# A three-buffer conditioning pipeline with interleaved context-projection blocks in the first stage

## The chip, the cores and the metric

The kernel runs on one core of a Trainium2 chip. The metric is the device time of one execution in microseconds (us): for the kernel before, the median of 3 runs is 3599.07 us (3596.9 to 3612.06). About 0.5% of that, 18 us, is what a comparison of this kernel can tell from no change.

## The reference, cut to what matters

The program computes two blocks of a network, one behind the other, in float32. Only the very beginning of the first block is touched by the change:

```python
def ada_params(cond, w, b):
    mod = jax.nn.silu(cond) @ w + b
    return jnp.split(mod, 3, axis=-1)
...
sh_l, sc_l, g_l = ada_params(c, ada_w[layer], ada_b[layer])
sh_c, sc_c, g_c = ada_params(c_ctx, ada_w[layer], ada_b[layer])
xm_l = x_lat * (1.0 + sc_l) + sh_l
xm_c = x_ctx * (1.0 + sc_c) + sh_c
...
proj = xm @ w_in        # of it, the first 512 columns of v belong to the first stage
```

Shift and scale (2048 each, for two conditioning vectors) come from a product with `ada_w` and are applied to the 256 tokens of `x` and the 256 of the context; then the modulated tokens are multiplied by `w_in`.

## The kernel before

**Precision and units.** All weights come from HBM in units of 1 MB (128 partitions x 2048 float32) through a ring of four slots, loaded by SyncE in a fixed order. A unit is used as two halves of 1024 columns. Each half is split into two parts that TensorE multiplies: ScalarE copies it, rounded, into `unit_hi` (`hb[b]`), VectorE writes what is left, ring minus `unit_hi`, into `unit_lo` (`lb[b]`). There are NBUF = 4 pairs of such buffers.

**The first stage.** It has 72 halves, listed in FIRST; x is a half's place in that list. 64 of them are conditioning halves ("A", called A0, A1, ... by their place x): two row blocks of `ada_w`, for which TensorE does four matmuls of 512 columns with the conditioning vectors as the stationary operand (`ada_half`, L799 and L801), into bank 4 or 5. The other eight are context halves ("L", called C30, C38, ... by their place): two row blocks of `w_in`'s v columns, 8 blocks of 128 x 128 each. For every block TensorE does six matmuls of 256 columns (`both_sets`, L824): tokens and context, and high and low parts, into banks 0 to 3. Before, the context halves stand at x = 30, 38, 47, 55 and 68 to 71.

**The chain of a group.** The conditioning comes in four groups of 4 x 128 features, 16 halves each. When a row of a group is complete, ScalarE copies it out of its bank (`ada_row`, L1393); with both there, TensorE turns the rows to columns (`ada_turn`, 16 weight loads and matmuls at L815, ahead of place ENDS[g] + 3, for the last group within a context half), VectorE adds the bias (`modulated`, L2045 and L2046), ScalarE applies scale and shift to four chunks of tokens and four of context (`x_scaled`, L1403), writes their high parts (`x_hi`, L1411), and VectorE their rests (`x_lo`, L1929). Only then may TensorE take the context halves of that group (semaphore `xm_lead`).

**What sets the order.** Every engine's program is written out by hand and runs in its own order; the engines meet in semaphores. ScalarE walks over x: for each half it waits for the ring's slot and for TensorE to be done with the buffer (`half_done`), then writes `unit_hi`. At fixed places the row copies, `x_scaled` and `x_hi` stand between. VectorE walks over x too: it waits for `hi_done` >= x + 1 and writes `unit_lo`, with `modulated` and `x_lo` at fixed places between. TensorE waits for `lo_done` >= x + 1 for the half x. Since these are counters, a half is ready only when all ahead of it in the list are split as well. In before, half x uses buffer x % 4, and `half_done` is raised by TensorE at the end of each half in the same order. SyncE loads a ring slot again when VectorE has written both rests of its unit. After the stage come the gates (two halves, 16 blocks in bank 7) and the rest of v, whose low parts GpSimd makes.

The line in ScalarE's helper that binds a half to the buffer's last user:

```python
for f in halves:
    b = (2 * n_static + f) % NBUF
    act.wait_ge(half_done, 2 * n + f + 1)
    act.activation(hb[b][:], ring[slot][:, f * HALF:(f + 1) * HALF], ACT.Copy).then_inc(hi_done, 1)
```

`half_done` starts at NBUF, so that half x waits for x - 4 to be done.

## Time and profile before

| | |
|---|---|
| median of 3 runs | 3599.07 us |
| lowest, highest | 3596.9, 3612.06 us |
| the profiled execution | 3602.43 us, of it the span 3600.6 us |
| TensorE (PE) busy | 3487.5 us, 97% |
| VectorE (DVE) busy | 2387.4 us, 66% |
| ScalarE (ACT) busy | 1619.1 us, 45% |
| GpSimd (POOL) busy | 1587.1 us, 44% |
| the first stage | from the start to 152 us |

Times in the views are microseconds from the start of the span. PE is TensorE's matmuls and PEld its weight loads; in the timeline an entry gives start, duration, engine, line of the source, output <- inputs, count, and in brackets how long the engine had been idle and what released it. A matmul's duration in these views is longer than the distance to the next one, since matmuls overlap; the distance of the starts is what a matmul costs. The granted clock (PEclk) is the share of TensorE's full 2.4 GHz.

### The profile page before, as it was taken

How to read it: one execution, taken by the hardware profiler on the slowest of the kernel's cores; microseconds unless marked ns; L12 is line 12 of the kernel's file. 1: busy time of each engine (PE TensorE's matmuls, PEld its weight loads, DVE VectorE, ACT ScalarE, POOL GpSimd, SP SyncE). 2: the span in 40 equal slices, each digit the busy share in tenths (PEclk: the TensorE clock that was granted, in tenths of full speed). 3: DMA queues.
4: the chain of work that ended last, by engine and by line, in shares of the span. 5: the costliest groups of instructions: out<-in, count | busy, mean ns of one | idle time of the engine just before them, and what ended most of it. 6: DMA issues, size and time to landing. Idle time of an engine off the chain costs nothing.

```text
span 3600.6 us, 65963 instructions
## 1 busy us (share of the span) xinstructions
PE 3487.5 (97%) x27080; PEld 3316.3 (92%) x27080; DVE 2387.4 (66%) x3663; ACT 1619.1 (45%) x2143; POOL 1587.1 (44%) x671
## 2 busy tenths in 40 slices
PE   7999998999999999999999999999999999999998
PEld 3799897979998989999999999999999899999998
DVE  7587466884545558364213779778888878788865
ACT  7513433333344444464444434444555444455553
POOL 0247592007264867826889980002333200133336
PEclk9999999999999999999999999999999999999999
DMA  9457661855564444545555555557888555688843
GB/s 354 191 225 265 268 238 59 327 208 213 223 223 147 164 153 148 204 164 188 185 190 196 190 180 195 188 184 256 318 304 313 183 196 197 239 323 302 314 175 129
DMA packets 118129, 784.66 MB, mean 218 GB/s; under 512 B 13488, under 2 KB 13616, under 8 KB 31920
## 3 DMA queue, kind: packets, MB, share of 16 engines
q1 hardware_dynamic: 97056, 703.65, 53.4%
q0 software_dynamic: 18832, 67.94, 4.8%
q10 hardware_dynamic: 2016, 9.87, 0.7%
q8 instruction: 165, 2.70, 0.3%
q14 instruction: 60, 0.49, 0.0%
HBM read 778.49 MB, written 2.10 MB: 217 GB/s over the span
## 4 chain that ended last, share of the span: by engine, by line
PE 83%; DVE 9%; POOL 2%; DMA 2%; ACT 2%; issue 2%; SPq 0%; DVEq 0%; ACTq 0%; POOLq 0%
PE bank L634 45%; PE bank L1236 12%; PE bank L652 6%; PE bank L1238 6%; PE bank L654 3%; DMA ring<-in_w 2%; POOL unit_lo L568 2%; PE bank L706 2%; PE bank L824 1%; PE bank L683 1%; ACT unit_hi L1328 1%; DVE ada_acc L1869 1%; PE bank L1184 1%; DVE unit_lo L1952 1%; PE bank L603 1%
## 5 line engine op out<-in xcount | busy, mean ns | idle before, releaser
L1328 ACT ACTIVATE unit_hi<-ring 128x1024 fp32r<-128x1024 f32 x1204 | 1248.2, 1057 | 1245.6 <-PE bank L634 429.0
L568 POOL TENSOR_TENSOR unit_lo<-ring,unit_hi 128x1024 fp32r<-128x1024 f32 x522 | 1337.8, 2584 | 962.0 <-ACT unit_hi L1328 961.0
L634 PE MATMUL bank<-x_parts,unit_hi 128*128 128x256 f32 (+1 forms) x7328 | 1306.8, 279 | 20.5 <-DVE unit_lo L1952 6.4
L634 PEld LDWEIGHTS bank<-x_parts,unit_hi 128*128 128x128 f32 x7328 | 1132.7, 190 | 27.9 <-issue 11.1
L634 PE MATMUL bank<-x_parts,unit_lo 128*128 128x256 f32 (+1 forms) x3664 | 1017.3, 278 | 0.0
L634 PEld LDWEIGHTS bank<-x_parts,unit_lo 128*128 128x128 f32 x3664 | 696.2, 190 | 0.0
L1236 PE MATMUL bank<-w_r,unit_hi 128*128 128x448 f32 x2048 | 647.4, 374 | 6.0 <-DVE w_r L2933 6.0
L1238 PE MATMUL bank<-w_r,unit_lo 128*128 128x224 f32 x2048 | 544.7, 266 | 0.0
L1236 PEld LDWEIGHTS bank<-w_r,unit_hi 128*128 128x128 f32 x2048 | 385.6, 188 | 38.0 <-DVE w_r L2933 3.8
L1238 PEld LDWEIGHTS bank<-w_r,unit_lo 128*128 128x128 f32 x2048 | 392.2, 192 | 0.0
L2848 DVE TENSOR_TENSOR unit_lo<-ring,unit_hi 128x1024 fp32r<-128x1024 f32 x256 | 313.4, 1225 | 99.9 <-ACT unit_hi L1328 90.9
L525 POOL DMA_INDIRECT pick<-in_ev,expert_idx x64 | 111.9, 1749 | 495.6 <-PE bank L1184 280.5
L652 PE MATMUL bank<-x_parts,unit_hi 128*128 128x448 f32 x1024 | 329.9, 380 | 0.0
L2741 DVE TENSOR_TENSOR unit_lo<-ring,unit_hi 128x1024 fp32r<-128x1024 f32 x224 | 270.6, 1221 | 86.4 <-ACT unit_hi L1328 86.0
L654 PE MATMUL bank<-x_parts,unit_lo 128*128 128x224 f32 x1024 | 271.2, 265 | 0.0
L525 POOL DMA_INDIRECT pick<-in_eu,expert_idx x64 | 116.0, 1812 | 238.9 <-DVE expert_dot L2860 203.2
L652 PEld LDWEIGHTS bank<-x_parts,unit_hi 128*128 128x128 f32 x1024 | 193.2, 189 | 17.1
L1869 DVE SCALAR_TENSOR_TENSOR ada_acc<-ring,cond,ada_acc 128x2048 f32<-128x2048 f32 x64 | 186.5, 2914 | 29.1 <-DMA ring<-in_w 27.8
L1952 DVE TENSOR_TENSOR unit_lo<-ring,unit_hi 128x1024 fp32r<-128x1024 f32 x130 | 153.4, 1221 | 76.0 <-ACT unit_hi L1328 75.6
L654 PEld LDWEIGHTS bank<-x_parts,unit_lo 128*128 128x128 f32 x1024 | 196.9, 192 | 0.0
L634 PE MATMUL bank<-ry_hi,unit_hi 128*128 128x256 f32 x480 | 133.0, 277 | 0.6 <-issue 0.6
L634 PE MATMUL bank<-ry_lo,unit_hi 128*128 128x256 f32 x480 | 132.6, 276 | 0.0
(484 smaller groups left out, 5782.1 us busy)
## 6 DMA issues: line engine op xcount, KB each, us to landing
ring<-in_w SPq DMA_DIRECT2D x669, 1024.0 KB, 4.9
resid<-in_xT ACTq DMA_DIRECT2D x4, 512.0 KB, 6.5
tmp_ctx<-in_ctxT ACTq DMA_DIRECT2D x4, 512.0 KB, 10.9
sgu_rows<-in_sgr ACTq DMA_DIRECT2D x1, 2048.0 KB, 10.3
rnn_gates<-in_rgw ACTq DMA_DIRECT2D x1, 2048.0 KB, 10.5
out<-resid SPq DMA_DIRECT2D x4, 512.0 KB, 2.6
pick<-in_eu,expert_idx POOLq DMA_INDIRECT x64, 8.0
pick<-in_ev,expert_idx POOLq DMA_INDIRECT x64, 8.1
```

The source lines that it names most:

```text
L525: pool.indirect_dma_start(slots[PICK_SLOT[k]][:], None, A[table][:, :], bass.IndirectOffsetOnAxis(ap=eidx[:, j:j + 1], axis=0), element_of ...
L568: pool.tensor_tensor(lb[b][:], ring[slot][:, f * HALF:(f + 1) * HALF], hb[b][:].bitcast(F32), ALU.subtract).then_inc(lo_done, 1)
L634: mm = pe.matmul(bank[(s.t0 + tile[m]) % TILES][:, 0:cols], w[b][:, (i % 8) * P:(i % 8 + 1) * P], mv[x][:, k, 0:cols], start=(k == 0 and w ...
L652: pe.matmul(two_parts(ps), hb[b][:, (k % 8) * P:(k % 8 + 1) * P], xb[:, :, k, 0:TM], start=(k == 0), stop=(k == KC - 1), skip_group_check= ...
L654: mm = pe.matmul(ps[:, 0:TM], lb[b][:, (k % 8) * P:(k % 8 + 1) * P], xb[:, 0, k, 0:TM], start=False, stop=(k == KC - 1), skip_group_check= ...
L1236: pe.matmul(two_parts(bank[c]), hb[b][:, c * P:(c + 1) * P], x[:], start=first, stop=False, skip_group_check=True)
L1238: return pe.matmul(bank[c][:, 0:TM], lb[b][:, c * P:(c + 1) * P], x[:, 0, :], start=False, stop=False, skip_group_check=True)
L1328: act.activation(hb[b][:], ring[slot][:, f * HALF:(f + 1) * HALF], ACT.Copy).then_inc(hi_done, 1)
L1869: dve.scalar_tensor_tensor(a[:], ring[u % RING][:], col, a[:], ALU.mult, ALU.add).then_inc(plain_done, 1)
L1952: dve.tensor_tensor(lb[b][:], ring[(s.u0 + s.npos[j]) % RING][:, f * HALF:(f + 1) * HALF], hb[b][:].bitcast(F32), ALU.subtract).then_inc(l ...
L2741: dve.tensor_tensor(lb[b][:], ring[(s.u0 + u) % RING][:, f * HALF:(f + 1) * HALF], hb[b][:].bitcast(F32), ALU.subtract).then_inc(lo_done, 1)
L2848: dve.tensor_tensor(lb[b][:], ring[(s.u0 + u) % RING][:, f * HALF:(f + 1) * HALF], hb[b][:].bitcast(F32), ALU.subtract).then_inc(lo_done, 1)
```

## The change

Four things are changed together, all within the first stage.

- The list FIRST: the context halves now stand at x = 28, 37, 46, 55, 64 and 69 to 71. The conditioning halves keep their order.
- The buffers: conditioning halves take turns in buffers 0, 1 and 2; the context halves at 28, 37, 46, 55, 64 and 71 all take buffer 3 (those at 69 and 70 take 1 and 2).
- TensorE's order: FIRST_PE lists its steps. When a context half is met, its eight blocks are put on a list, and behind each following conditioning half TensorE takes one block from it; what is left is done at the end. The eight halves of `[C28]` so lie behind A29 to A36, those of C37 behind A38 to A45, and so on; C64 has four blocks behind A65 to A68 and four after them. The last turn stands ahead of C69's first block.
- The waits on `half_done` follow: FIRST_DONE says as which TensorE completes a half, and `first_buffer_free(x)` which count the buffer's last user gives. ScalarE waits for that count.

The diff, cut to its core:

```diff
-FIRST = (ADA[:30] + [("L", 0, 0, 0)] + ADA[30:37] + [("L", 0, 0, 1)] + ADA[37:45] + [("L", 1, 0, 0)]
-         + ADA[45:52] + [("L", 1, 0, 1)] + ADA[52:] + [("L", g, 0, f) for g in (2, 3) for f in range(2)])
+LEADS = {28: (0, 0), 36: (0, 1), 44: (1, 0), 52: (1, 1), 60: (2, 0)}
+FIRST = []
+for _i, _a in enumerate(ADA):
+    if _i in LEADS:
+        FIRST.append(("L",) + (LEADS[_i][0], 0, LEADS[_i][1]))
+    FIRST.append(_a)
+FIRST += [("L", 2, 0, 1), ("L", 3, 0, 0), ("L", 3, 0, 1)]
+FIRST_BUF, _n = [], 0
+for _kind, _g, _i, _f in FIRST:
+    FIRST_BUF.append(_n % 3 if _kind == "A" else {(2, 1): 1, (3, 0): 2}.get((_g, _f), 3))
+    _n += _kind == "A"
+FIRST_PE, _open = [], []
+for _x, _h in enumerate(FIRST):
+    if _h[0] == "L":
+        _open += [(_x, _i) for _i in range(8 * _h[3], 8 * _h[3] + 8)]
+        continue
+    FIRST_PE.append((_x, None))
+    if _open:
+        FIRST_PE.append(_open.pop(0))
+FIRST_PE += _open
+_last = {_x: _k for _k, (_x, _) in enumerate(FIRST_PE)}
+FIRST_DONE = {_x: _n + 1 for _n, _x in enumerate(sorted(_last, key=_last.get))}
+def first_buffer_free(x):
+    before = [y for y in range(x) if FIRST_BUF[y] == FIRST_BUF[x]]
+    return FIRST_DONE[before[-1]] if before else 0
+TURN_LAST = (2, 8)
...
-            for x, (kind, g, i, f) in enumerate(FIRST):
-                u = x % NBUF
+            for x, part in FIRST_PE:
+                kind, g, i, f = FIRST[x]
+                u = FIRST_BUF[x]
...
-                for i in range(8 * f, 8 * f + 8):
-                    if g == 2 and i == 2:
-                        ada_turn(3)
...
+                if (g, part) == TURN_LAST:
+                    ada_turn(3)
+                mm = both_sets(bank[part % 4], (hb, lb), u, part, (xl, xc), GR * g + part // 4,
+                               g == 0 and part < 4, g == 3 and part >= 12)
+                if part % 8 == 7:
+                    mm.then_inc(half_done, 1)
...
-                            act.wait_ge(half_done, NBUF + ROW_END[g][b] + 1)
+                            act.wait_ge(half_done, NBUF + FIRST_DONE[ROW_END[g][b]])
...
+                    act.wait_ge(half_done, NBUF + first_buffer_free(x))
```

**TensorE, where a context half's blocks end.** Before, TensorE's row at the last matmuls of C30 (buffer 2), the conditioning half A31 (buffer 3) and the start of A32 (buffer 0):

```order
L824 MATMUL bank3<-x_parts_72,unit_hi2_55 128x256
L824 MATMUL bank3<-xc_lo_74,unit_hi2_55 128x256
L824 MATMUL bank3<-x_parts_72,unit_lo2_59 128x256
L824 MATMUL bank3<-xc_hi_73,unit_lo2_59 128x256
L799 MATMUL bank4<-unit_hi3_56,cond_parts_104 4x512 [waits lo_done]
L801 MATMUL bank4<-unit_lo3_60,cond_parts_104 2x512
L799 MATMUL bank4<-unit_hi3_56,cond_parts_104 4x512
L801 MATMUL bank4<-unit_lo3_60,cond_parts_104 2x512
L799 MATMUL bank4<-unit_hi0_53,cond_parts_104 4x512 [waits lo_done]
```

After, TensorE's row at the last block of C28 (buffer 3), A38 (buffer 0) and the first block of C37 (buffer 3 again):

```order
L861 MATMUL bank3<-x_parts_72,unit_hi3_56 128x256
L861 MATMUL bank3<-xc_lo_74,unit_hi3_56 128x256
L861 MATMUL bank3<-x_parts_72,unit_lo3_60 128x256
L861 MATMUL bank3<-xc_hi_73,unit_lo3_60 128x256
L836 MATMUL bank4<-unit_hi0_53,cond_parts_104 4x512 [waits lo_done]
L838 MATMUL bank4<-unit_lo0_57,cond_parts_104 2x512
L836 MATMUL bank4<-unit_hi0_53,cond_parts_104 4x512
L838 MATMUL bank4<-unit_lo0_57,cond_parts_104 2x512
L861 MATMUL bank0<-x_parts_72,unit_hi3_56 128x256 [waits lo_done]
L861 MATMUL bank0<-xc_hi_73,unit_hi3_56 128x256
```

Before, the context half's end is followed by halves whose buffers were free all along; now it is followed by A38, which stands behind C37 in the list of halves, and C37 goes into the buffer that has just been read.

**ScalarE, at the same place.** Before, ScalarE's row at x = 36 to 39 (C38 is the one in buffer 2), with the loads of tokens and the first scaling of group 1:

```order
L1328 ACTIVATE unit_hi0_53<-ring2_51 128x1024 [waits half_done,slot_loaded2]
L1433 DMA resid_61<-in_xT 128x1024
L1434 DMA tmp_ctx_75<-in_ctxT 128x1024
L1328 ACTIVATE unit_hi1_54<-ring2_51 128x1024 [waits half_done,slot_loaded2]
L1328 ACTIVATE unit_hi2_55<-ring3_52 128x1024 [waits half_done,slot_loaded3]
L1328 ACTIVATE unit_hi3_56<-ring3_52 128x1024 [waits half_done,slot_loaded3]
L1403 ACTIVATE tmp_lat_76<-resid_61,mod_64 128x256 [waits x_in1,mod_ready]
```

After, the same stretch of ScalarE (C37 is the one in buffer 3):

```order
L1469 ACTIVATE unit_hi2_55<-ring2_51 128x1024 [waits half_done,slot_loaded2]
L1479 DMA resid_61<-in_xT 128x1024
L1480 DMA tmp_ctx_75<-in_ctxT 128x1024
L1469 ACTIVATE unit_hi3_56<-ring2_51 128x1024 [waits half_done,slot_loaded2]
L1469 ACTIVATE unit_hi0_53<-ring3_52 128x1024 [waits half_done,slot_loaded3]
L1469 ACTIVATE unit_hi1_54<-ring3_52 128x1024 [waits half_done,slot_loaded3]
L1443 ACTIVATE tmp_lat_76<-resid_61,mod_64 128x256 [waits x_in1,mod_ready]
```

The length and kind of the row are the same; the context half has moved ahead by one place and waits for `half_done` of C28 where C38 waited for that of A34.

**ScalarE, at the end of the stage.** Before, ScalarE's row at x = 69 to 71, with the copy of the last conditioning row:

```order
L1328 ACTIVATE unit_hi1_54<-ring2_51 128x1024 [waits half_done,slot_loaded2]
L1328 ACTIVATE unit_hi2_55<-ring3_52 128x1024 [waits half_done,slot_loaded3]
L1393 ACTIVATE ada_rows_103<-bank5 4x512 [waits half_done]
L1328 ACTIVATE unit_hi3_56<-ring3_52 128x1024 [waits half_done,slot_loaded3]
L1403 ACTIVATE tmp_lat_76<-resid_61,mod_64 128x256 [waits x_in3,mod_ready]
```

After:

```order
L1469 ACTIVATE unit_hi1_54<-ring2_51 128x1024 [waits half_done,slot_loaded2]
L1469 ACTIVATE unit_hi2_55<-ring3_52 128x1024 [waits half_done,slot_loaded3]
L1469 ACTIVATE unit_hi3_56<-ring3_52 128x1024 [waits half_done,slot_loaded3]
L1433 ACTIVATE ada_rows_103<-bank5 4x512 [waits half_done]
L1443 ACTIVATE tmp_lat_76<-resid_61,mod_64 128x256 [waits x_in3,mod_ready]
```

The row copy (`ada_rows`), which stood ahead of the high part of x = 71, now stands behind it, and that half now takes buffer 3, which C64 holds.

## Rows read from the trace of the kernel before

**Rows 1.** The page: the span; busy time, share of the span, instructions of TensorE.

```profile
span 3600.6 us, 65963 instructions
...
PE 3487.5 (97%) x27080; PEld 3316.3 (92%) x27080; DVE 2387.4 (66%) x3663; ACT 1619.1 (45%) x2143; POOL 1587.1 (44%) x671
```

**Rows 2.** Timeline of the last turn and the end of the stage, engine by engine.

```profile
128.04 0.49 PE L815 MATMUL bank<-con,ada_rows 4*128 4x4 f32 x3
...
130.03 0.17 DVE L2045 SCALAR_TENSOR_TENSOR mod<-bank,vec 128x8 f32<-128x8 f32 x1 [0.34 <-PE bank L815]
...
130.82 2.07 ACT L1403 ACTIVATE tmp_lat<-resid,mod 128x256 f32<-128x256 f32 x4 [2.39 <-DVE tick L2020]
...
137.05 1.22 DVE L1929 TENSOR_TENSOR xc_lo<-tmp_ctx,xc_hi 128x1024 fp32r<-128x1024 f32 x1
...
152.26 1.06 ACT L1328 ACTIVATE unit_hi<-ring 128x1024 fp32r<-128x1024 f32 x1 [4.32 <-PE bank L824]
```

**Rows 3.** Windows: us, busy us per engine, granted clock, DMA share, GB/s.

```profile
20.00:40.00 20.00, 14.21 (x64) 5.09 (x64) 14.59 (x18) 14.20 (x16) 0.00 (x0) 1.00 1.01 415
...
80.00:100.00 20.00, 16.88 (x90) 8.80 (x88) 15.01 (x14) 12.64 (x14) 0.00 (x0) 0.91 0.77 289
```

**Rows 4.** Waits, 0 to 150 us (SyncE's own last): total us, times, longest.

```profile
DVE unit_lo L2062 <- ACT unit_hi L1328: 31.9, 22, 4.3
...
ACT unit_hi L1328 <- PE bank L824: 17.9, 5, 5.0
...
ACT unit_hi L1328 <- PE bank L801: 10.6, 10, 1.9
...
SPq L463 <- DVE unit_lo L2062: 114.3, 36, 6.4
```

**Rows 5.** Chain that ended last: start us, us, engine, line, count.

```profile
67.28 1.87 PE bank L815 x16
...
104.15 5.46 PE bank L824 x48
```

**Rows 6.** Timeline of TensorE from C30's last matmul into A31.

```profile
63.29 0.28 PE L824 MATMUL bank<-xc_hi,unit_lo 128*128 128x256 f32 x1
63.41 0.40 PE L799 MATMUL bank<-unit_hi,cond_parts 128*4 128x512 f32 x1
...
64.33 0.40 PE L799 MATMUL bank<-unit_hi,cond_parts 128*4 128x512 f32 x1
```

**Rows 7.** Timeline of ScalarE and VectorE after C47 ended at 95.65.

```profile
95.75 1.06 ACT L1328 ACTIVATE unit_hi<-ring 128x1024 fp32r<-128x1024 f32 x1 [4.38 <-PE bank L824]
...
96.71 1.04 ACT L1328 ACTIVATE unit_hi<-ring 128x1024 fp32r<-128x1024 f32 x1
...
96.84 5.78 DVE L2062 TENSOR_TENSOR unit_lo<-ring,unit_hi 128x1024 fp32r<-128x1024 f32 x5 [4.21 <-ACT unit_hi L1328]
```

**Rows 8.** Timeline of group 1's scaling (ScalarE) and rests (VectorE).

```profile
71.22 2.06 ACT L1403 ACTIVATE tmp_lat<-resid,mod 128x256 f32<-128x256 f32 x4
...
79.90 1.99 ACT L1328 ACTIVATE unit_hi<-ring 128x1024 fp32r<-128x1024 f32 x2
...
80.97 1.23 DVE L2062 TENSOR_TENSOR unit_lo<-ring,unit_hi 128x1024 fp32r<-128x1024 f32 x1 [0.67 <-ACT unit_hi L1328]
...
84.39 8.24 DVE L2062 TENSOR_TENSOR unit_lo<-ring,unit_hi 128x1024 fp32r<-128x1024 f32 x7
```

**Rows 9.** Timeline around the first turn: ScalarE, and TensorE's A18.

```profile
37.14 1.04 ACT L1328 ACTIVATE unit_hi<-ring 128x1024 fp32r<-128x1024 f32 x1
38.79 1.06 ACT L1328 ACTIVATE unit_hi<-ring 128x1024 fp32r<-128x1024 f32 x1 [0.60 <-PE bank L801]
...
37.61 0.40 PE L799 MATMUL bank<-unit_hi,cond_parts 128*4 128x512 f32 x1
```

**Rows 10.** Windows of 3.4 us, columns as in Rows 3.

```profile
83.20:86.60 3.40, 1.09 (x5) 0.25 (x4) 3.40 (x4) 2.01 (x3) 0.00 (x0) 0.98 0.84 308
86.60:90.00 3.40, 3.40 (x9) 1.11 (x9) 3.40 (x4) 2.12 (x2) 0.00 (x0) 0.52 0.61 200
```

More of the change, by code:

```diff
@@ L136 @@
 NFIRST = len(FIRST) // 2
+for _b in range(4):
+    assert max(FIRST_DONE[_x] for _x in range(2 * NFIRST) if FIRST_BUF[_x] == _b) <= 2 * NFIRST - 3 + _b
+TURN_LAST = (2, 8)
 class Stage:
@@ L829, in _ @@
             pe.wait_ge(S("cond_lo"), 1)
-            for x, (kind, g, i, f) in enumerate(FIRST):
-                u = x % NBUF
-                for turned in range(NG - 1):
-                    if x == ENDS[turned] + 3:
-                        ada_turn(turned)
-                if kind == "L" and f == 0:
-                    pe.wait_ge(S("xm_lead"), 2 * g + 2)
-                pe.wait_ge(lo_done, x + 1)
+            for x, part in FIRST_PE:
+                kind, g, i, f = FIRST[x]
+                u = FIRST_BUF[x]
                 if kind == "A":
+                    for turned in range(NG - 1):
+                        if x == ENDS[turned] + 3:
+                            ada_turn(turned)
+                    pe.wait_ge(lo_done, x + 1)
                     ada_half(u, g, i, f)
                     continue
-                for i in range(8 * f, 8 * f + 8):
-                    if g == 2 and i == 2:
-                        ada_turn(3)
-                    mm = both_sets(bank[i % 4], (hb, lb), u, i, (xl, xc), GR * g + i // 4,
-                                   g == 0 and i < 4, g == 3 and i >= 12)
-                mm.then_inc(half_done, 1)
+                if part % 8 == 0:
+                    if f == 0:
+                        pe.wait_ge(S("xm_lead"), 2 * g + 2)
+                    pe.wait_ge(lo_done, x + 1)
+                if (g, part) == TURN_LAST:
[4 more added lines that the diff above has]
+                    mm.then_inc(half_done, 1)
             n = PLAN["gates"].n0
@@ L1425, in _ @@
                 u = s0.u0 + x // 2
-                hi(x // 2, (u % RING, u // RING + 1, x // 2), (x % 2,))
+                if x < 2 * NFIRST:
+                    act.wait_ge(slot_loaded[u % RING], 16 * (u // RING + 1))
+                    act.wait_ge(half_done, NBUF + first_buffer_free(x))
+                    act.activation(hb[FIRST_BUF[x]][:], ring[u % RING][:, x % 2 * HALF:(x % 2 + 1) * HALF], ACT.Copy
+                                   ).then_inc(hi_done, 1)
+                else:
+                    hi(x // 2, (u % RING, u // RING + 1, x // 2), (x % 2,))
                 if x == 4:
@@ L2059, in _ @@
                 if x < 2 * NFIRST:
-                    b = x % NBUF
+                    b = FIRST_BUF[x]
                     dve.wait_ge(hi_done, x + 1)
```

## Prediction

> **What bounds the kernel now.** Halves are named by their place x in FIRST: A27 is a conditioning half, C30 a context half of eight blocks. TensorE is busy 97% of the span [rows 1], but the edit touches only the first stage, which ends when the last context half is done: the instruction of ScalarE that waits for it starts at 152.26 [rows 2]. So I read the first 152 us and ask who ends each wait there. In the window from 80 to 100 us TensorE is busy 16.88 of 20 us, DMA at 0.77 [rows 3]: neither is full. In the waits, ScalarE waits 17.9 us for TensorE's context blocks, 10.6 us for its conditioning matmuls, and VectorE 31.9 us for ScalarE [rows 4]. SyncE waits 114.3 us for VectorE to free a slot of the ring: the loads are ahead. The three engines' waits are one loop: TensorE frees a buffer, ScalarE writes its high part, VectorE the rest, TensorE uses it. While TensorE is in a context half the loop stands still for four buffers.
>
> The prices. A context half is 48 matmuls in 5.46 us, so 0.68 us for a block of six, and a turn of rows to columns 1.87 us [rows 5]. A conditioning half is four matmuls 0.23 us apart, 0.92 us, and passing from a block to it costs nothing: 63.29 to 63.41 is a block matmul's own spacing [rows 6]. After a context half ends, the high part starts 0.1 us later and the next 0.96 us after it; VectorE starts 1.1 us after the first and goes on every 1.15 us [rows 7].
>
> Check of these prices on before. From C30 at 57.68 TensorE has 34 conditioning halves (31.3 us), 64 blocks (43.5) and 3 turns (5.6) left: 80.4 us, so 138.1 without any wait. It is done at 152.2. The 14.1 us between are all that a perfect interleave could give back, half-rate clock included.
>
> **The change part by part.** *Interleaving.* TensorE's work is the same; per pair it has 0.92 + 0.68 = 1.60 us, above VectorE's 1.15 and ScalarE's 0.95 for a half. With three buffers for conditioning, a freed one is wanted again 2 x 0.92 + 3 x 0.68 = 3.9 us later, and needs 0.1 + 1.06 + 1.2 = 2.4 us. So inside a run of pairs there is no wait, and the 5 us standstill goes.
>
> *The one buffer for context halves.* This is what I think decides. C37 may be written only when C28's last block is done, and TensorE's order puts that block directly ahead of A38 (the order fence of TensorE). ScalarE takes its instructions in order, so C37's high part and everything behind it (A38, A39, the scalings of group 1) stand still until then; VectorE then splits C37 first, and only then A38. TensorE has nothing else queued but A38. Its hole, by [rows 7]: 0.1 to the high part, 1.1 to the first rest, 2 x 1.15 for both rests: 3.5 us. It occurs at x = 37, 46, 55 and 64, since each context half stands directly behind the end of the one before. At 37 and 55 the sums of `modulated` stand between the two rests, 0.8 us from the first of them to ScalarE's next [rows 2]: 4.3 us there. Sum of holes: 2 x 3.5 + 2 x 4.3 = 15.6 us. In before the same waits were covered by three conditioning halves that were ready.
>
> *ScalarE's scalings, behind the holes at 37 and 55.* They cannot begin before `modulated`, 3.2 us after TensorE's last block. ScalarE's row shows 71.22 for the first scaling and 79.90 for the high part of the half ahead of which the last scaled parts went: 8.7 us [rows 8]. VectorE starts that half's rest at 80.97, then two rests of x, and the next half's rest at 84.39, done at 85.6 [rows 8]; so that is 14.4 us after the first scaling, 17.6 after the last block. Here that is the rest of A44. TensorE, from 4.3 on, has A38 to A43 with six blocks, 9.6 us, to 13.9; so it waits 3.6 us in all on A41 to A44. Before had this too (its loss is in the 14.1), hidden in part by C38. Twice: 7.2 us. Each piece of nine halves from 37 thus takes 17.6 + 2 x 1.6 = 20.8 us, that from 46 (no scaling) 3.5 + 8 x 1.6 + 1.9 = 18.2.
>
> *The tail.* The last conditioning half, A68, now has 5 blocks of C64 behind it. C71 goes into the context buffer too, so its high part waits for C64's end, and on ScalarE the row copy that the last turn needs stands behind C71 (the order fence of ScalarE): 0.1 + 0.95 + 0.6 = 1.7 us of waiting TensorE before the turn. From the turn's start x's rests are ready at 137.05 + 1.22 - 128.04 = 10.2 us [rows 2]; TensorE covers 1.9 + 8 x 0.68 = 7.3 of them with the turn and C69, and waits 2.9 us before C70. Before it had two whole context halves there and no wait. Tail: 4.6 us.
>
> *Three buffers instead of four ahead of x = 28.* There ScalarE waits mostly for DMA, and a cycle of three buffers (1.06 + 1.2 + 0.92 + 0.1 = 3.3 us, 1.1 a half) is still under the 1.26 us in which a half of 0.52 MB arrives at 415 GB/s [rows 3]. The exception is the first turn: A18 comes behind it at 37.61 and ends 0.92 later, at 38.5; with four buffers only A22's high part waited for it, 0.60 us, with three it is A21's, which began at 37.14 [rows 9] and now does at 38.6. The scaling chain behind starts 0.8 us later. Bounds: 0, if VectorE's own queue is what ends last, and 1.5, the whole shift of A21; I take 0.8.
>
> *The start.* A29 is split one cadence (1.15 us) ahead of what was C30: 56.5, with the 0.8 57.3.
>
> Sum for the stage: 57.3 + 36 x 0.92 (33.1) + 64 x 0.68 (43.5) + 3 x 1.87 (5.6) = 139.5, plus waits 15.6 + 7.2 + 4.6 = 27.4: 166.9. Against 152.2: **+14.7 us**, at full clock.
>
> *The clock.* From 83.2 to 86.6 TensorE was busy 1.09 of 3.40 us at a granted 0.98; from 86.6 to 90 it got 0.52, half of 2.4 GHz [rows 10]. At half rate 3.4 us of work lose 1.7. Such costs of before are in its 14.1. After, there are four holes of 3.5 to 4.3 us. Behind those at 37 and 55 the later waits (3.6) take up the loss; behind those at 46 and 64 TensorE is the bound and 1.7 us is lost each; behind the tail's hole I count half of one, 0.8. That is 4.2 us; bounds 0 (none falls on paced work) and 8.5 (five of them).
> The Trainium skill ("TensorE: Matmul & The Clock Gate", "Why this matters for your kernels") says that a longer idle gap between bursts of matmuls sends the clock back to half rate. By that rule, this change, which keeps TensorE fed in small bites but opens four gaps, pays it every time. The row at 83.2 to 90 agrees with it; that every gap of this size does it, no run here shows yet.
>
> After the stage all is released from TensorE's last block, as in before, where VectorE's and ScalarE's next steps stand at 152.26 [rows 2], and the weight ring is full in before [rows 4] and, drained more slowly, in the changed kernel too. So I carry the delay on in full. Forecast: 14.7 + 4.2 = **+18.9 us**. The profiled execution was 3602.43 us (span 3600.6), the median 3599.07; from the median this gives **3618**.
>
> **The rivals.**
> 1. *Holes, but no cost of the clock:* 14.7 us, 3614. For it: from 80 to 100 us, with gaps of several us on TensorE, the clock was still 0.91 in the mean [rows 3], so only some gaps cost anything. Against: [rows 10], where one did.
> 2. *Half rate after every gap, on work that paces:* five stretches of 1.7, 14.7 + 8.5 = 23.2, 3622. For it: the gaps here, with what is light around them, are as bare as the stretch of [rows 10]. Against: the holes at 37 and 55 have slack behind them. The rule of the Trainium skill above would lead here.
> 3. *Not slower: the holes are covered.* If the new context half's high part did not keep ScalarE from running ahead (its buffer free before A38 is wanted), the 15.6 us and some of the scaling waits go. The stage is then 139.5 + 4.6 to 139.5 + 11.8: 144 to 151, that is 1 to 8 us faster, 3591 to 3598. It decides where the last block of a context half stands: one half earlier than the next context half would do. In before the loop's standstill (17.9 us) is real, which speaks for a gain; the order, with no half between, speaks against.
> 4. *Absorbed later:* part of the delay is taken up behind the stage. GpSimd has its first splits earlier than needed there. But they were ready in time before too, so a delay of the whole can't be hidden; if half of it were, 3608.
> 5. *The buffers of x < 28 matter more than I think:* the ring is starved once or twice for want of a freed slot and every later load is late by a half's 1.26 us or two each time, +3 to +5 on top: 3622.
>
> **How the numbers follow.** Forecast (3616 to 3620) 0.45; rival 1 0.25; rivals 2 and 5 0.17; rival 4 0.07; rival 3 0.06. A measurement here can tell about 0.5% (18 us: below 3581 or above 3617) from no change, and my forecast lies just at that bound. Slower by over 0.5%: 0.7 of the forecast (0.31) and rivals 2 and 5 (0.17), 0.48. Within: 0.50. Faster by over 0.5%: even without any wait the stage gives 14 us, so 0.02. The range must hold rival 1 and reach into 2 and 4: 3608 to 3627.
>
> **What would show it.** Four gaps of 3.5 to 4.4 us before a conditioning half on TensorE, each with ScalarE waiting for a block of TensorE just ahead of a high part in the context buffer; the waits of ScalarE for context blocks fewer and shorter than 17.9 us; stage end at 165 to 172 instead of 152.3; a wait of about 3 us before C70; a granted clock near 0.5 in stretches behind the gaps. It is wrong if conditioning halves follow at those four places without a gap (rival 3), if the stage ends at 167 with a clock of 1.0 (rival 1), or if the stage's delay is not found in the total (rival 4).

## The result and the profile after

The changed kernel took **3622.56 us** (median of 6 runs, 3618.64 to 3630.69), the kernel before 3600.81 us in 6 runs beside it: 21.8 us slower, ratio 1.0061 with a 95% interval of 1.0048 to 1.0075. The profiled execution of the changed kernel, 3630.69 us with a span of 3628.8, is the slowest of its six; before's was 3602.43. Places in a trace are those of one execution.

In the section on the change, "the eight halves of C28" behind A29 to A36 are its eight blocks; C28 is one half.

The instructions that answer to the end of the stage: VectorE's copy out of the banks, behind TensorE's last block. Timeline of VectorE, first kernel before, then after; columns as in the timelines above:

```profile
152.26 2.74 DVE L2068 COPY vstage<-bank 128x256 f32<-128x256 f32 x8 [13.99 <-PE bank L824]
```

```profile
175.55 2.74 DVE L2114 COPY vstage<-bank 128x256 f32<-128x256 f32 x8 [11.67 <-PE bank L861]
```

The stage ends 23.3 us later; in before it is the same moment as the instruction of ScalarE at 152.26 in [rows 2]. Then the delay goes through the kernel. One later place, of before and of after, from the views of one source line (instruction and count, duration least/median/most in ns, first and last start):

```profile
L706 PE MATMUL bank<-unit_hi,x_parts x256: 388/392/581, 737.2 to 827.9; 128*128 128x512 f32 x128
```

```profile
L743 PE MATMUL bank<-unit_hi,x_parts x256: 387/392/586, 769.4 to 860.2; 128*128 128x512 f32 x128
```

It is 32.2 us later there, and 28.2 at the end of the span. Nothing is taken up; the few microseconds between these figures are within what single executions of one kernel differ by.

TensorE in the stage, after: every wait of 1 us or more in the 36 pairs, the last turn, and the wait before C70. In brackets how long TensorE stood idle before it and for whom.

```profile
57.32 0.59 PE L836 MATMUL bank<-unit_hi,cond_parts 128*4 128x512 f32 x1 [1.19 <-DVE unit_lo L2108]
...
79.93 0.40 PE L836 MATMUL bank<-unit_hi,cond_parts 128*4 128x512 f32 x1 [4.78 <-DVE unit_lo L2108]
...
92.72 0.39 PE L836 MATMUL bank<-unit_hi,cond_parts 128*4 128x512 f32 x1 [1.32 <-DVE unit_lo L2108]
...
99.70 0.39 PE L836 MATMUL bank<-unit_hi,cond_parts 128*4 128x512 f32 x1 [3.60 <-DVE unit_lo L2108]
...
120.75 0.40 PE L836 MATMUL bank<-unit_hi,cond_parts 128*4 128x512 f32 x1 [4.39 <-DVE unit_lo L2108]
...
133.93 0.39 PE L836 MATMUL bank<-unit_hi,cond_parts 128*4 128x512 f32 x1 [1.63 <-DVE unit_lo L2108]
...
140.91 0.39 PE L836 MATMUL bank<-unit_hi,cond_parts 128*4 128x512 f32 x1 [3.60 <-DVE unit_lo L2108]
...
153.68 1.92 PE L852 MATMUL bank<-con,ada_rows 4*128 4x4 f32 x16 [1.73 <-issue]
...
163.94 0.38 PE L861 MATMUL bank<-x_parts,unit_hi 128*128 128x256 f32 x1 [0.98 <-DVE xc_lo L1975]
```

The four holes stand before A38, A47, A56 and A65. What makes the first of them is read on the two other engines; timeline of ScalarE and VectorE, after (C28's last matmul starts at 74.88):

```profile
75.25 2.95 ACT L1469 ACTIVATE unit_hi<-ring 128x1024 fp32r<-128x1024 f32 x3 [6.45 <-PE bank L861]
76.34 1.23 DVE L2108 TENSOR_TENSOR unit_lo<-ring,unit_hi 128x1024 fp32r<-128x1024 f32 x1 [6.28 <-ACT unit_hi L1469]
...
78.65 2.36 DVE L2108 TENSOR_TENSOR unit_lo<-ring,unit_hi 128x1024 fp32r<-128x1024 f32 x2 [0.42 <-DVE tick L2066]
```

ScalarE stood 6.45 us at C37's high part, for TensorE's block of C28, with A38's behind it. VectorE then splits C37 (76.34), does group 1's `modulated`, and only from 78.65 splits A38, which TensorE takes at 79.93. In [rows 7] the same restart took place with TensorE still fed. The later four of this kind, ScalarE's high parts of C46, C55, C64 and C71, after:

```profile
96.20 3.90 ACT L1469 ACTIVATE unit_hi<-ring 128x1024 fp32r<-128x1024 f32 x4 [5.83 <-PE bank L861]
...
116.46 2.95 ACT L1469 ACTIVATE unit_hi<-ring 128x1024 fp32r<-128x1024 f32 x3 [6.45 <-PE bank L861]
...
137.41 3.90 ACT L1469 ACTIVATE unit_hi<-ring 128x1024 fp32r<-128x1024 f32 x4 [5.83 <-PE bank L861]
...
152.05 1.06 ACT L1469 ACTIVATE unit_hi<-ring 128x1024 fp32r<-128x1024 f32 x1 [4.09 <-PE bank L861]
```

Each follows 0.1 us behind the end of a context half, so they cut the stage into **pieces**: 20.95, 20.26, 20.95 and 14.64 us, and 23.5 from the last to the copy at 175.55. The experiments are read by these pieces.

The waits from 0 to 150 us, after (those of [rows 4]):

```profile
ACT unit_hi L1469 <- PE bank L861: 24.6, 4, 6.5
...
SPq L500 <- DVE unit_lo L2108: 132.4, 35, 8.8
```

And the clock, windows of after, columns as in [rows 3]: the start of the pairs, the hole before A38, what follows it, what follows the holes before A47, A56 and A65, and the last turn with C69.

```profile
57.00:63.40 6.40, 6.08 (x21) 3.87 (x22) 3.80 (x5) 2.40 (x3) 0.00 (x0) 0.50 1.01 407
...
74.50:80.00 5.50, 0.72 (x7) 0.53 (x6) 3.12 (x8) 4.69 (x7) 0.00 (x0) 1.00 0.32 107
80.00:84.00 4.00, 4.00 (x14) 2.30 (x15) 2.23 (x2) 4.00 (x7) 0.00 (x0) 0.57 0.91 320
...
100.90:104.60 3.70, 3.70 (x17) 2.57 (x16) 2.25 (x2) 1.95 (x2) 0.00 (x0) 0.54 0.84 325
...
121.00:124.00 3.00, 3.00 (x12) 1.94 (x11) 2.06 (x2) 3.00 (x7) 0.00 (x0) 0.56 0.93 358
142.00:145.50 3.50, 3.50 (x16) 2.40 (x15) 2.35 (x2) 1.47 (x2) 0.00 (x0) 0.53 0.91 356
154.00:160.00 6.00, 6.00 (x40) 5.98 (x40) 1.00 (x6) 3.58 (x8) 0.00 (x0) 0.72 0.53 178
```

Each of the four holes is followed by a stretch near 1.2 GHz (0.5 of full). A shorter one follows the wait of 1.73 us before the last turn: the 0.72 of the last row is the mean of 6 us, and 3 of these, from 155.7 to 158.7, ran at 0.50. The four holes agree with the rule of the Trainium skill that the prediction weighed ("TensorE: Matmul & The Clock Gate", "Why this matters for your kernels"). The wait of 1.73 us is shorter than the gaps that it speaks of.

### The profile page after: what moved, and what is told of

Read it like the earlier page. It is cut to its first block, busy times and chain, and to the rows that moved or that the text cites. A ratio compares the mean times of both kernels' runs of the same rounds, so it can differ in the third digit from the quotient of the medians.

```text
span 3628.8 us, 65963 instructions
## 1 busy us (share of the span) xinstructions
PE 3499.3 (96%) x27080; PEld 3330.2 (92%) x27080; DVE 2384.0 (66%) x3663; ACT 1619.6 (45%) x2143; POOL 1585.0 (44%) x671
## 4 chain that ended last, share of the span: by engine, by line
PE 83%; DVE 9%; ACT 2%; POOL 2%; issue 2%; DMA 2%; DVEq 0%; SPq 0%; ACTq 0%; POOLq 0%
PE bank L671 46%; PE bank L1276 11%; PE bank L689 6%; PE bank L1278 6%; PE bank L691 3%; POOL unit_lo L605 2%; DMA ring<-in_w 2%; PE bank L743 2%; PE bank L861 1%; PE bank L720 1%; PE bank L1224 1%; DVE ada_acc L1915 1%; DVE unit_lo L2108 1%; PE bank L640 1%; DVE unit_lo L1998 1%
## 5 line engine op out<-in xcount | busy, mean ns | idle before, releaser
L1368 ACT ACTIVATE unit_hi<-ring 128x1024 fp32r<-128x1024 f32 x1132 | 1174.9, 1058 | 1213.3 <-PE bank L671 432.6
L671 PEld LDWEIGHTS bank<-x_parts,unit_hi 128*128 128x128 f32 x7328 | 1135.7, 191 | 27.7 <-issue 10.9
```

The source lines that it names most:

```text
L671: mm = pe.matmul(bank[(s.t0 + tile[m]) % TILES][:, 0:cols], w[b][:, (i % 8) * P:(i % 8 + 1) * P], mv[x][:, k, 0:cols], start=(k == 0 and w ...
```

## The experiments

All are compared with runs of the kernel before on the same chip; these had medians of 3600.81 to 3603.89 us, so it is the ratios that compare. "Stage end" is the start of the copy `vstage`, 152.3 in before and 175.6 in the changed kernel. It is read from one execution of each: the changed kernel and e7, one program up to the last row copy, differ by 2.2 us in one piece of the stage and by 0.9 the other way in another. So 2 or 3 us in this column alone show nothing. A change of order or of buffers is made on the changed kernel.

| kernel | order | buffers for A + for C | stage end, us | median, us | ratio to before, 95% |
|---|---|---|---|---|---|
| before | eight in a row | 4 shared | 152.3 | 3600.81 | 1 |
| changed | one block a half | 3 + 1 | 175.6 | 3622.56 | 1.0061 (1.0048 to 1.0075) |
| e1 | one block | 3 + 2 | 155.5 | 3606.01 | 1.0017 (1.0006 to 1.0028) |
| e2 | two blocks | 3 + 1 | 159.8 | 3609.72 | 1.0023 (1.0011 to 1.0034) |
| e3 | one block, holes filled, 14 fillers | 3 + 1 | 176.6 | 3632.15 | 1.0084 (1.0065 to 1.0102) |
| e5 | one block | 4 + 1 | 171.4 | 3621.16 | 1.0051 (1.0033 to 1.0069) |
| e6 | one block, holes filled, 8 fillers | 3 + 1 | 169.9 | 3624.15 | 1.0065 (1.0046 to 1.0083) |
| e7 | one block, row copy first | 3 + 1 | 173.8 | 3625.23 | 1.0066 (1.0043 to 1.0089) |
| e8 | eight in a row | 3 + 1 | 167.5 | 3619.20 | 1.0043 (1.0026 to 1.0060) |
| e9 | one block, C68 to C71 at the end | 4 + 2 | 149.3 | 3600.52 | 0.9989 (0.9978 to 1.0000) |
| e10 | eight in a row | 4 + 1 | 150.9 | 3605.18 | 1.0001 (0.9992 to 1.0010) |

**A second context buffer (e1).** A fifth pair of buffers lies where nothing else is live in this stage; C37 and C55 use it.

```diff
-    FIRST_BUF.append(_n % 3 if _kind == "A" else {(2, 1): 1, (3, 0): 2}.get((_g, _f), 3))
+    FIRST_BUF.append(_n % 3 if _kind == "A" else {(2, 1): 1, (3, 0): 2, (0, 1): 4, (1, 1): 4}.get((_g, _f), 3))
...
+        hb.append(zone("unit_hi4", 98, [P, HALF], F32R))
+        lb.append(zone("unit_lo4", 102, [P, HALF], F32R))
```

> The changed kernel with a second buffer pair for context halves: C28, C46, C64 in buffer 3, C37 and C55 in a new buffer 4; conditioning halves stay in three, TensorE's order is untouched. Theory (the single buffer makes ScalarE hold up everything behind a context half until the one before is read): no idle stretch of 3.6 to 4.8 us ahead of A38, A47, A56 and A65; the 16.4 us of them go, and with them one or two of the half-rate stretches behind (1.6 us each): the stage ends at 155 to 160 us instead of 175.5, the whole takes 3602 to 3607 us. Rival 1 (three buffers for conditioning halves are too few) and rival 2 (taking blocks one by one is what costs, by its switching or by the clock): the stage still ends at 172 to 176, the whole stays at 3618 to 3625.

The stage ended at 155.5. TensorE of e1; the waits behind the first two context halves; 1.08 and 1.62 stand once more at 111.89 and 119.09, and none else of 1 us or more between 60 and 125:

```profile
80.19 0.39 PE L838 MATMUL bank<-unit_hi,cond_parts 128*4 128x512 f32 x1 [1.08 <-DVE unit_lo L2110]
...
87.39 0.39 PE L838 MATMUL bank<-unit_hi,cond_parts 128*4 128x512 f32 x1 [1.62 <-DVE unit_lo L2110]
```

No hole is left, and the stage ends 20.1 us before that of the changed kernel (about 1 of these is the start: the first turn of the pairs, group 1's, is at 68.92 instead of 69.89). In this order the single context buffer made the holes, not the interleaving as such.

**Two blocks a half (e2).** The blocks of a context half are done after four conditioning halves, so that its buffer is free four halves before the next wants it.

```diff
-    if _open:
-        FIRST_PE.append(_open.pop(0))
+    FIRST_PE += _open[:2]
+    del _open[:2]
```

> The changed kernel with its buffers, but TensorE takes two blocks behind a conditioning half, not one, so that a context half is read through four conditioning halves ahead of the next one. Theory: the buffer is free 3.7 us of work earlier, which is as long as the hole: holes gone, the stage ends at 155 to 161, the whole 3602 to 3608 us. Rival 1 (three conditioning buffers): 3618 to 3625, since nothing of that changes. Rival 2 (small bites): part of it at most, 3612 to 3620.

Stage end 159.8, 15.8 us less than the changed kernel: the holes go with the one buffer kept. That is the second way to the same end, and shows that the hold time of the buffer decides. The total, 3609.7, lies above the 3602 to 3608 expected. The waits that stay between 70 and 130 us are six, of 0.6 to 2.3 us.

**Fillers in the holes (e3, then e6).** Before the wait of A38, A47, A56 and A65 TensorE multiplies constants into a bank that nobody reads: 14 times in e3, 8 times in e6.

```diff
+                    if x in (38, 47, 56, 65):
+                        keep(14, 7)
                     pe.wait_ge(lo_done, x + 1)
```

> The changed kernel with 14 matmuls of no use (256 columns, about 0.22 us each at full clock, 3.1 us) into the unused bank 7 ahead of TensorE's waits for A38, A47, A56 and A65: they fill the holes and change no buffer. Theory, its clock term: the half-rate stretches behind these holes (0.57 at 80 to 84, 0.54 at 100.9 to 104.6, 0.53 at 142 to 145.5) go; behind A47 and A65 they are on the path with 1.6 us each, so the stage ends 3 us earlier, at 172 to 173, and the whole takes 3618 to 3620 us instead of 3622.6. If the clock costs nothing there: no change. If the matmuls last longer than the hole: slower.

The 14 took 5.9 us, 0.42 each, where I had counted on 0.22; the holes are 3.6 to 4.8, so the fillers overran them. TensorE of e3, and two windows behind the fillers (columns as above):

```profile
74.97 6.21 PE L819 MATMUL bank<-con 128*128 128x256 f32 x28
80.82 0.58 PE L836 MATMUL bank<-unit_hi,cond_parts 128*4 128x512 f32 x1
```

```profile
80.00:84.00 4.00, 4.00 (x24) 2.76 (x23) 2.22 (x2) 4.00 (x7) 0.00 (x0) 1.00 0.87 330
...
100.00:105.00 5.00, 5.00 (x29) 3.65 (x28) 2.66 (x3) 1.37 (x3) 0.00 (x0) 1.00 0.86 315
```

The clock stays at 1.00 where the changed kernel had 0.57 and 0.54, with the same work there: the idle time ahead had sent it down. In time e3 settles little, since the overrun ate the gain: its pieces are 20.95, 20.98, 20.97 and 15.36 us. Its median is 31 us above before for a stage that ends 24.3 later; the interval of its ratio begins at 23.4 us, and whether there is more than scatter behind the stage stays open. So the fillers were cut to 8.

> As the run with 14 useless matmuls, but with 8: one measured 0.42 us there, so 14 of them (5.9 us) overran the hole by 1 to 2 us each, while the work behind them ran at a full clock. 8 are 3.4 us, within the holes of 3.6 and 4.4 to 4.8 us. Theory, its clock term: all four stretches behind the holes run at full clock and cost 1.1 to 1.6 us less each, also behind A38 and A56, where the prediction had counted on slack: the stage ends at 169 to 172 us instead of 175.5, the whole takes 3615 to 3619 us. If the clock term is only the 3 us predicted: 172 to 173, 3619. If the clock falls all the same: 175, 3622.

With 8, TensorE waits 1.33 us behind the fillers of A38 and 0.94 behind those of A56, and not at all behind the other two. The clock is 1.00 from 60 to 140 us; one window, and ScalarE's high parts of C37, C46, C55, C64 and C71 in e6:

```profile
120.00:140.00 20.00, 17.06 (x97) 11.49 (x96) 13.41 (x13) 12.82 (x15) 0.00 (x0) 1.00 0.62 229
```

```profile
73.03 2.95 ACT L1471 ACTIVATE unit_hi<-ring 128x1024 fp32r<-128x1024 f32 x3 [6.45 <-PE bank L861]
...
94.02 3.90 ACT L1471 ACTIVATE unit_hi<-ring 128x1024 fp32r<-128x1024 f32 x4 [5.86 <-PE bank L861]
...
112.74 2.95 ACT L1471 ACTIVATE unit_hi<-ring 128x1024 fp32r<-128x1024 f32 x3 [6.45 <-PE bank L861]
...
133.70 3.90 ACT L1471 ACTIVATE unit_hi<-ring 128x1024 fp32r<-128x1024 f32 x4 [5.84 <-PE bank L861]
...
146.78 1.06 ACT L1471 ACTIVATE unit_hi<-ring 128x1024 fp32r<-128x1024 f32 x1 [4.09 <-PE bank L861]
```

The pieces are 20.99, **18.72**, 20.96 and **13.08**. Those with a scaling (from C37 and from C55) are as long as with the half rate, 20.95: there the scalings' chain sets the length and the loss of the clock is hidden. The other two are shorter by 1.54 and 1.56 us: what a drop cost in these executions where nothing hides it (e7, further down, has a dearer one). This is what the prediction had said of each; the expectation above, which hoped for a gain behind A38 and A56 too, was wrong. The stage ends at 169.9, 5.7 us earlier: 3.1 from these two pieces, 0.4 from the last, and 2.2 that are there at 73.03 already, ahead of any filler. So it is by luck that 169.9 falls into the 169 to 172 expected. The total doesn't show it: 3624.15 was measured where 3615 to 3619 was expected, and by the interval (17 to 30 us above before) it is no better than the changed kernel (17 to 27).

**Four conditioning buffers (e5).** Is it the third or the fourth buffer of the conditioning halves that matters?

```diff
-    FIRST_BUF.append(_n % 3 if _kind == "A" else {(2, 1): 1, (3, 0): 2}.get((_g, _f), 3))
+    FIRST_BUF.append(_n % 4 if _kind == "A" else {(2, 1): 1, (3, 0): 2, (3, 1): 3}.get((_g, _f), 4))
```

(and the fifth pair of e1)

> The changed kernel with four buffers (0 to 3) for conditioning halves and a fifth, new one for C28, C37, C46, C55 and C64; the last three context halves take 1, 2 and 3. TensorE's order is untouched. Theory: the holes stay at 3.6 to 4.8 us, since the context halves still share one buffer; what goes is 0.8 us at the first turn and the 1.7 us ahead of the last turn (C71's high part waits for A68, not for C64): the stage ends 2 to 4 us earlier than 175.5, the whole takes 3617 to 3621. Rival 1 (three buffers are too few): most of the loss goes, 3600 to 3608.

TensorE of e5 at the holes:

```profile
76.86 0.59 PE L838 MATMUL bank<-unit_hi,cond_parts 128*4 128x512 f32 x1 [4.78 <-DVE unit_lo L2110]
...
96.66 0.59 PE L838 MATMUL bank<-unit_hi,cond_parts 128*4 128x512 f32 x1 [3.60 <-DVE unit_lo L2110]
```

The four holes are 4.78, 3.60, 4.39 and 3.60 us, the same to the hundredth. They ask only when the context buffer comes free, not how many the others have. The stage ends 4.2 us earlier. Its start gives 3.1 of these (group 1's turn is at 66.77 instead of 69.89), but only about 1 by the buffer: a conditioning half waited for at 55.05 in the changed kernel begins at 54.10. The rest is the clock of the first pairs (0.93 from 57.0 to 60.2, for 0.50), which e7 will show to differ between executions. The wait before the last turn, which e5 doesn't have, gives more, and the piece from C37's end to C46's takes some back (21.15 us for 20.26).

**The row copy ahead of C71 (e7).**

```diff
-                        if x == ROW_END[g][b] + 4:
+                        if x == min(ROW_END[g][b] + 4, 2 * NFIRST - 1):
```

> The changed kernel, but ScalarE's copy of the last conditioning row stands ahead of C71's high part, not behind it, as in the kernel before. Theory: TensorE's idle 1.73 us ahead of the last turn goes, the wait ahead of C70 grows by some tenths since VectorE has C71's rest to write first; the stage ends 1 to 1.7 us earlier, at about 174 us, too little for the total to show (3621). Rival: the copy was not what ended last there, and the 1.73 us stay.

TensorE's wait of 1.73 before the last turn is gone, and that before C70 is 3.09 instead of 0.98. From A65 to the stage's end it takes 34.25 us (139.59 to 173.84) where the changed kernel takes 34.64 (140.91 to 175.55). The row copy did gain something: C70 begins 10.6 us after C64's end (161.15) instead of 12.0 (163.94). But C70 and C71 then take 12.7 us instead of 11.6, for the clock falls behind the longer wait; windows from C70 on, first e7, then the changed kernel:

```profile
161.10:164.60 3.50, 3.45 (x17) 3.46 (x18) 0.00 (x0) 0.37 (x1) 3.50 (x2) 0.54 0.00 0
```

```profile
163.90:167.40 3.50, 3.46 (x29) 3.47 (x30) 0.00 (x0) 0.35 (x1) 3.50 (x2) 1.00 0.00 0
```

So removing the first wait made the second long enough to cost 1.1 of the 1.4 us gained. The stage end is 1.7 us earlier, as expected, but by luck. Only 0.4 of it is the tail; the wait before C70 grew by 2.1 us and not by tenths.

The rest lies ahead, where e7 and the changed kernel are one program. At C28's end e7 is 2.2 us earlier (73.00 against 75.25 in ScalarE's row). Windows of e7 in the first pairs, where the changed kernel has 0.50 from 57.0 to 63.4:

```profile
57.00:60.20 3.20, 2.97 (x14) 1.54 (x15) 2.57 (x4) 1.96 (x2) 0.00 (x0) 0.77 1.00 415
60.20:63.40 3.20, 3.20 (x22) 2.16 (x21) 2.41 (x3) 2.12 (x2) 0.00 (x0) 1.00 1.02 397
```

From C37's end to C46's it loses 0.9: that piece takes 21.16 us for 20.26. ScalarE of e7 at C46 and C55, then the 6.8 us behind the hole before A47 in e7 and in the changed kernel:

```profile
93.96 3.90 ACT L1469 ACTIVATE unit_hi<-ring 128x1024 fp32r<-128x1024 f32 x4 [5.38 <-PE bank L861]
...
115.12 2.95 ACT L1469 ACTIVATE unit_hi<-ring 128x1024 fp32r<-128x1024 f32 x3 [6.45 <-PE bank L861]
```

```profile
97.40:104.20 6.80, 6.74 (x25) 4.13 (x26) 4.20 (x5) 2.57 (x3) 0.00 (x0) 0.60 0.79 306
```

```profile
99.70:106.50 6.80, 6.80 (x32) 4.47 (x33) 4.67 (x4) 3.31 (x4) 0.00 (x0) 0.75 0.82 298
```

One program, two executions: how long the half rate lasts is not fixed. Here it made 2.2 us at the start of the pairs, and one drop cost 2.44 us instead of 1.54 (against e6's 18.72).

**The buffers alone, with before's order (e8, then e10).** Order and places of before, eight blocks in a row; conditioning halves in three buffers and the own context buffer.

```diff
+FIRST = (ADA[:30] + [("L", 0, 0, 0)] + ADA[30:37] + [("L", 0, 0, 1)] + ADA[37:45] + [("L", 1, 0, 0)]
+         + ADA[45:52] + [("L", 1, 0, 1)] + ADA[52:] + [("L", g, 0, f) for g in (2, 3) for f in range(2)])
...
-        _open += [(_x, _i) for _i in range(8 * _h[3], 8 * _h[3] + 8)]
+        FIRST_PE += [(_x, _i) for _i in range(8 * _h[3], 8 * _h[3] + 8)]
...
-TURN_LAST = (2, 8)
+TURN_LAST = (2, 2)
```

> One part of the change alone: conditioning halves in three buffers, context halves in a buffer of their own (C30, C38, C47, C55, C68 and C71 in 3, C69 and C70 in 1 and 2), but at the places of before, and TensorE takes their eight blocks in a row. Theory: no hole, since at least seven conditioning halves lie between two context halves; from the three buffers 0.8 us at the first turn and up to 1 us for each of four context halves (three halves are ready behind it, not three and the fourth being made), and 1 us at the end, where C71 waits for C68: the stage ends at 153 to 158 us, the whole takes 3601 to 3607. Rival 1 (three buffers for conditioning halves cost the most): 3612 or more.

This expectation was plainly wrong: the stage ended at 167.5. So three buffers and one cost 15.2 us in before's order too, without a wait of TensorE above 2.3 us ahead of the last turn; interleaving on top of them cost 8.1 more. e10 adds the fourth conditioning buffer (FIRST_BUF and fifth pair as in e5), which also gives C71 another buffer than C68's; nothing else changes.

> The places and the order of the kernel before (eight blocks of a context half in a row), conditioning halves in four buffers (0 to 3), and a fifth buffer of its own for the context halves C30, C38, C47, C55 and C68; C69, C70 and C71 take buffers 1, 2 and 3. It differs from e8_own_buffer_alone by the number of conditioning buffers alone (and so in where C71 goes).
> Theory A, the loss of e8 came from three conditioning buffers (the whole context half of 5.5 us then has only two or three split halves ready behind it) and from C71 sharing the context buffer with C68: with a fourth the waits of TensorE behind each context half go back to those of the kernel before or below, ScalarE waits no more than 17.9 us for context blocks, C71 waits for A67 alone, and the stage ends at 148 to 152 us; 0 to 4 us faster than before, 3597 to 3603.
> Theory B, a buffer that only context halves use costs something of its own in the order of before: the stage ends at 158 to 168 as in e8, 3606 to 3620.

Stage end 150.9, ratio 1.0001: theory A of e10, though its median of 3605.2 is above the 3597 to 3603 expected. TensorE of e8 (last turn, C70), and ScalarE of e8 at C71; then e10's last turn and stage end:

```profile
135.32 1.94 PE L844 MATMUL bank<-con,ada_rows 4*128 4x4 f32 x16
...
153.81 0.58 PE L853 MATMUL bank<-x_parts,unit_hi 128*128 128x256 f32 x1 [5.18 <-DVE xc_lo L1967]
```

```profile
143.28 1.06 ACT L1461 ACTIVATE unit_hi<-ring 128x1024 fp32r<-128x1024 f32 x1 [8.91 <-PE bank L853]
```

```profile
125.98 1.94 PE L846 MATMUL bank<-con,ada_rows 4*128 4x4 f32 x16
...
150.91 2.74 DVE L2108 COPY vstage<-bank 128x256 f32<-128x256 f32 x8 [14.71 <-PE bank L855]
```

Of the 16.5 us between them, 9.3 are there at the last turn (135.32 to 125.98), and 2.6 of these at group 1's turn. Between the two turns TensorE's waits of 0.5 us or more sum to 9.6 us in e8, most of them of 0.6 to 0.8 us, and to 5.2 in e10; the 2.3 us that are left were not traced. ScalarE's waits for conditioning matmuls, 0 to 160 us, e8 and then e10:

```profile
ACT unit_hi L1461 <- PE bank L830: 28.2, 19, 5.3
```

```profile
ACT unit_hi L1463 <- PE bank L832: 17.9, 10, 6.0
```

The other 7.2 are the tail, where e10 has also moved C71 to another buffer: in e8 C71's high part waits 8.91 us for C68, the scaling behind it starts late, and TensorE waits 5.18 us before C70. With one block a half the third buffer costs little (e5), as the prediction had it; with eight in a row, it comes back from a context half and takes the ready halves at 0.92 us each, faster than the two engines make them (1.15 us, [rows 7]). That one more half in store is what saves the 9.3 us is argued from this; that the fourth buffer saves most of them is shown, since 9.3 is well above what two executions of one program differ by.

**Everything relieved (e9).** Four conditioning buffers, two context buffers in turn, interleaving for the first four context halves, and the last four behind the last conditioning half as in before.

```diff
-LEADS = {28: (0, 0), 36: (0, 1), 44: (1, 0), 52: (1, 1), 60: (2, 0)}
+LEADS = {28: (0, 0), 36: (0, 1), 44: (1, 0), 52: (1, 1)}
...
-    FIRST_BUF.append(_n % 3 if _kind == "A" else {(2, 1): 1, (3, 0): 2}.get((_g, _f), 3))
+    FIRST_BUF.append(_n % 4 if _kind == "A" else {(3, 0): 2, (3, 1): 3}.get((_g, _f), 4 + _f))
```

(two more pairs of buffers, `cond_parts` at another place, TURN_LAST back to (2, 2))

> A version meant to beat both: four buffers for conditioning halves, two new ones for context halves taking turns, one block behind each conditioning half from A29 to A63 as in the change, but C68 to C71 all behind the last conditioning half and the last turn behind two blocks of C68, as in before. Theory: no holes, no wait at the end of the stage; what stays are the waits for ScalarE's scalings (two of 1.1 and 1.6 us per group, 5.4 us in the run with two context buffers) and some half-rate time: 138.7 + 5.4 + 3 to 6 = 147 to 150 us for the stage, 3596 to 3600 us for the whole against 3601 before. Rival 2 (small bites cost in themselves): no earlier than before, 152 us or more.

```profile
149.30 2.74 DVE L2116 COPY vstage<-bank 128x256 f32<-128x256 f32 x8 [13.31 <-PE bank L863]
```

3 us before the kernel before, with all that the idea can have, and at a ratio of 0.9989 (0.9978 to 1.0000) a gain of 0 to 8 us. e10, without interleaving, ends 1.4 us before it. Both are within what two executions of one program differ by, so no gain from interleaving is shown. With the buffers there it is harmless.

## Why the prediction held, and where its steps did not

The prediction's sum, cut at the same places as the pieces (its numbers: 57.3 for A29; 14.67 for eight pairs and a turn; 20.8; 18.2 + 1.7 of clock; 20.8; 3.5 + 9.1 + 1.7; and 1.7 + 10.2 + 10.9 + 0.8 to the end), in us:

| piece | predicted | changed kernel | e7 (same program up to the tail) | e6 (holes filled) |
|---|---|---|---|---|
| to A29 | 57.3 | 57.3 | 57.2 | 57.2 |
| A29 to the end of C28 | 14.7 | 17.8 | 15.7 | 15.7 |
| C28's end to C37's | 20.8 | 20.95 | 20.96 | 20.99 |
| C37's to C46's | 19.9 | 20.26 | 21.16 | 18.72 |
| C46's to C55's | 20.8 | 20.95 | 20.97 | 20.96 |
| C55's to C64's | 14.3 | 14.64 | 14.53 | 13.08 |
| C64's end to the stage's | 23.6 | 23.5 | 23.2 | 23.1 |
| stage | 171.3 | 175.5 | 173.8 | 169.9 |

(The prediction's own total is 166.9 + 4.2 = 171.1; the pieces sum to a little more by rounding.)

- **The holes (right, and shown).** Four at the four places named: 4.78, 3.60, 4.39 and 3.60 us, 16.4 where 15.6 was said, each with ScalarE standing at a context half's high part. e1 and e2 take them away with a second context buffer or a shorter hold, e5 keeps them with a fourth conditioning buffer. Rival 3 (holes covered) is false for this kernel; e1 and e2 are what it would have looked like.
- **The scalings' waits and the clock behind A38 and A56 (right as a sum).** 3.6 us a group were said at full clock, and 1.32 and 1.63 were waited. But A44 came at 92.72, 17.6 us after C28's end, as said: the wait is shorter by the clock's loss and by a hole 0.5 longer, both of which the chain hides. The pieces of 20.95 are the proof, with e6's.
- **The clock behind A47 and A65 (right).** 1.7 us each were said. Against e6 the changed kernel lost 1.54 and 1.56, and e7 2.44 and 1.45. So rival 1 (no cost of the clock) is false, and rival 2 too, though its 3622 is the measured time: half rate came after every hole, but two of four are hidden.
- **The start (the step that failed).** From A29 to C28's end 14.7 us were said and 17.8 taken: at 57.0 to 63.4 the clock is 0.50. I had priced these pairs at full clock because no hole stands ahead. In before the same stretch is C30's 48 dense matmuls and ran at 1.00. The term that was missing is shown by the clock rows; that the change of order put it there is not. From 57.0 to 60.2 the interleaved kernels have 0.50 (e2, e9), 0.60 (e1), 0.70 (e3), 0.75 (e6), 0.77 (e7) and 0.93 (e5); those with eight blocks in a row have 1.00 (before, e10) and 0.52 (e8). Every one of them has half rate somewhere between 46 and 63 us, before too (0.71 from 50 to 54), and what it costs depends on the work it falls on. A29 to C28's end is 15.7 us in e6 and e7 and 17.8 here, with the same program. So 1 us of the 3.1 is in all three executions, and 2.1 is in how this one fell.

The window of C30 in before, for that:

```profile
57.68:63.41 5.73, 5.73 (x49) 5.70 (x49) 3.26 (x3) 1.02 (x1) 0.00 (x0) 1.00 1.01 379
```

- **The tail (right as a sum, in one term by luck).** 1.73 us before the turn is the 1.7. Of the 2.9 before C70 only 0.98 were waited, since C69 ran at half rate meanwhile (0.72 from 154 to 160): turn and C69 took 9.3 us for 7.3. C70 began 10.26 us after the turn, where 10.2 was said: the rests of x set it, as predicted. The 0.8 us of clock counted behind the wait before C70 is not there: the clock was 1.00 from 163.9. C70 and C71 took 11.5 us all the same, for 10.9; the 0.6 stays open. That a longer wait there does cost clock is in e7, 1.1 us.
- **Four conditioning buffers or three (right, in this order).** A21's high part began at 38.71, said 38.6, and e5 has its conditioning halves 0.95 us earlier, where 0.8 was said. Its holes are unchanged. But that holds for the order of the changed kernel alone: in the order of before e8 ended 16.5 us behind e10, 9.3 of it ahead of the last turn, and no rival had that.
- **"Fewer and shorter than 17.9 us" (wrong).** ScalarE's waits for context blocks are fewer, 4 instead of 5, but longer: 24.6 us in the window of [rows 4], single ones 6.5 instead of 5.0. Interleaving was to remove the standstill; it moved it to the buffer's next user. The argument on the holes implied as much, and the list of signs contradicted it.
- **Carried on in full (right).** +23.3 us in the stage, +28.2 in the span, +21.8 in the medians. Rival 4 is false. Rival 5's place (the loads) is not where the time went: the ring's waits grew to 132.4 us from 114.3, so the loads are further ahead than before.

So the stage of this execution was said 4.2 us too short, of which 3.1 are the start, and 2.1 of these chance. In the medians +18.9 us was said and +21.8 measured.

## What to carry to other kernels

When work is spread out to let a pipeline breathe, count for how long each buffer is now held, and who wants it next: a half read in eight bites held its buffer for about 15 us (C37's from 81.22 to 96.10) instead of 5.5, and the next writer stood on an in-order engine ahead of everything else. A second buffer cured it, and so did bites twice as large. The most that could be won here was 14.1 us, and the best version (e9) won 0 to 8. Sharing one buffer cost 20 us, 16.4 of it in four holes. And test each part alone: three buffers for conditioning halves, nearly free with one block a half, were not free with eight in a row.
